# Cross attention of both layers: the last two query units and the four output units as seven products, one quarter of the output per unit

## What is computed

```python
def memory_cross_attention(h, mem_k, mem_v, wq, wo):
    q = (h @ wq).reshape(B, S, XATTN_HEADS, XATTN_HEAD_DIM)      # 4 heads of 256
    s = jnp.einsum('bshd,bmhd->bhsm', q, mem_k) * (XATTN_HEAD_DIM ** -0.5)
    p = jax.nn.softmax(s, axis=-1)
    o = jnp.einsum('bhsm,bmhd->bshd', p, mem_v).reshape(B, S, C)
    return o @ wo

for i in range(2):
    x = x + 0.5 * swiglu_ffn(rms_norm(x, ffn1_norm[i]), ...)
    h = rms_norm(x, mix_norm[i])
    x = x + (rwkv7_time_mix(h, ...) if i == 0 else gmlp_chunk_mix(h, ...))
    x = x + memory_cross_attention(rms_norm(x, xattn_norm[i]), mem_k, mem_v, wq[i], wo[i])
    x = x + 0.5 * swiglu_ffn(rms_norm(x, ffn2_norm[i]), ...)
```

## Time and profile before

| | us |
|---|---|
| median of 3 runs | 2095.15 |
| lowest and highest | 2095.09 and 2101.4 |
| the profiled execution, its own time | 2102.88 |
| its span in the trace | 2101.1 |
| TensorE busy | 2035.8 (97%) |
| VectorE busy | 1080.4 (51%) |
| ScalarE busy | 374.5 (18%) |
| GpSimd busy | 947.2 (45%) |

### The profile page before, as it was taken

How to read it: one execution, slowest core, us unless ns; L and a number is a source line. 1 busy time by engine, 2 the same in 40 slices (tenths; PEclk the granted TensorE clock), 3 DMA queues, 4 the chain that set the end, 5 groups by cost and what they waited for, 6 DMA issues and landing times.

```text
span 2101.1 us, 38775 instructions
## 1 busy us (share of the span) xinstructions
PE 2035.8 (97%) x16734; PEld 1900.8 (90%) x16734; DVE 1080.4 (51%) x1882; ACT 374.5 (18%) x769; POOL 947.2 (45%) x725
## 2 busy tenths in 40 slices
...
DMA packets 43588, 307.61 MB, mean 146 GB/s; under 512 B 5128, under 2 KB 5384, under 8 KB 7328
## 3 DMA queue, kind: packets, MB, share of 16 engines
...
## 4 chain that ended last, share of the span: by engine, by line
PE 92%; DVE 6%; issue 1%; ACT 1%; DMA 0%; SPq 0%; DVEq 0%; ACTq 0%
PE ps L541 53%; PE ps L252 16%; PE ps L304 8%; PE ps L249 3%; PE ps L266 3%; PE ps L281 1%; PE ps L1586 1%; DVE sb_xn L2406 1%; PE ps L360 1%; PE ps L1565 0%; DVE sb_xn L407 0%; PE ps L2135 0%; DMA sb_ring<-stream 0%; PE ps L2120 0%; PE ps L1991 0%
## 5 line engine op out<-in xcount | busy, mean ns | idle before, releaser
L541 PE MATMUL ps<-sb_work,sb_ring 128*128 128x128 f32 x3648 | 438.6, 275 | 2.0 <-DVE sb_work L1842 2.0
L541 PEld LDWEIGHTS ps<-sb_work,sb_ring 128*128 128x128 f32 x3648 | 423.1, 192 | 2.2 <-POOL sb_table L512 2.2
L512 POOL TENSOR_TENSOR sb_pad<-sb_ring 128x512 f32<-128x512 f32 x59 | 75.5, 1279 | 485.7 <-issue 318.9
L512 POOL TENSOR_TENSOR sb_table<-sb_ring 128x512 f32<-128x512 f32 x118 | 151.0, 1280 | 261.4 <-PE ps L541 152.6
L541 PE MATMUL ps<-sb_work,sb_table 128*128 128x128 f32 x2096 | 266.7, 275 | 0.0
L541 PEld LDWEIGHTS ps<-sb_work,sb_table 128*128 128x128 f32 x2096 | 250.6, 193 | 0.0
L515 POOL TENSOR_TENSOR sb_ring<-sb_ring 128x512 f32<-128x512 f32 x177 | 244.3, 1380 | 0.0
L541 PE MATMUL ps<-sb_xn,sb_ring 128*128 128x128 f32 x1376 | 167.7, 275 | 0.0
L514 POOL TENSOR_TENSOR sb_table<-sb_table,sb_ring 128x512 f32<-128x512 f32 x118 | 161.4, 1368 | 9.3
L304 PE MATMUL ps<-sb_work,sb_ring 128*128 128x256 f32 x736 | 160.1, 380 | 5.4 <-issue 1.9
L304 PEld LDWEIGHTS ps<-sb_work,sb_ring 128*128 128x128 f32 x736 | 139.4, 190 | 26.5 <-issue 4.4
...
## 6 DMA issues: line engine op xcount, KB each, us to landing
...
```

Source lines behind the costliest of these rows:

```text
L512: v.tensor_tensor(s[:, 0], a[1][0], a[1][1], ALU.add).then_inc(S["fw_ready"], 1)
L541: ins = mm(fast_bank(c, g, b)[:, i * P:i * P + P], *(sides[::-1] if token_major else sides), start=first and i == 0 and j == 0, stop=last ...
```

## The change

In each of the two layers, query units 2 and 3 and all four output units become fast units. The plan counts two banks instead of four for the queries. The list of stages that GpSimd prepares gets `l0_x` between `l0_ffn1` and `l0_ffn2`, and `l1_x` between `gm` and `l1_ffn2`; six units each. On VectorE, `spread_input` on `xn` now stands ahead of `rescaled`, and two `fast_sum` ahead of the first maximum; ScalarE makes two `copy_first` in place of two copies of a bank. Behind the last head VectorE makes for each head three differences of its output (`spread`, L1695, L1697 and L1699 of the changed kernel), written to `work[5]`. The output weights are cut the other way: each unit holds all 1024 inputs for 256 of the outputs, so a quarter of the result is complete with each unit, and `fast_residual` (L718) takes the place of `add_residual`: its sum in SBUF is added to `c.h` in SBUF.

```diff
@@ FAST_ORDER, fast_counts
-FAST_ORDER = ["b2_ffn", "l0_ffn1", "l0_ffn2", "l1_ffn1", "gm", "l1_ffn2"]
+FAST_ORDER = ["b2_ffn", "l0_ffn1", "l0_x", "l0_ffn2", "l1_ffn1", "gm", "l1_x", "l1_ffn2"]
...
+        elif name in ("l0_x", "l1_x"):
+            start, units, outs = PLAN[name + "q"][0] + 2, 6, 6
@@ fast_residual
+        if f is None and name != "gm_out":
+            c.wait_done(dve, PLAN[name][0] + b)
@@ xattn_tensor
     for u in range(2, 4):
-        p_unit(c, pe, n0 + u, q0 + u, c.xn)
+        pe.wait_ge(S["fw_ready"], 4 * (z0 + u - 2) + 4)
+        pe.wait_ge(S["fast_read"], g0 + u - 3)
+        fast_products(c, pe, n0 + u, z0 + u - 2, range(4),
+                      lambda k, j, t: c.xn[:, 2 * k + j, t * P:t * P + P], lambda k, m: xt[:, m, k, :],
+                      g0 + u - 2, True, True,
+                      (lambda: pe.wait_ge(S["spread"], x_count(i) + 4)) if u == 2 else None)\
+            .then_inc(S[f"unit_done{(n0 + u) % UNITS}"], 1)
...
                 pe.wait_ge(S["x_o_read"], 4 * i + hd - 1)
+                pe.wait_ge(S["spread"], x_count(i) + 4 + 3 * (hd - 2) + 3)
...
     pe.wait_ge(S["x_o_read"], 4 * i + 4)
+    pe.wait_ge(S["spread"], x_count(i) + 13)
     for u in range(4):
-        d_unit(c, pe, n0 + u, lambda k: W[1][:, 2 * u + k, :], u == 0, u == 3)
+        z, g = z0 + 2 + u, g0 + 2 + u
+        pe.wait_ge(S["fw_ready"], 4 * z + 4)
+        pe.wait_ge(S["fast_read"], g - 1)
+        fast_products(c, pe, n0 + u, z, range(4),
+                      lambda k, j, t: W[1][:, 2 * k + j, t * P:t * P + P],
+                      lambda k, m: x_spread(c, k)[:, m * P:m * P + P], g, True, True,
+                      (lambda: pe.wait_ge(S["spread"], x_count(i) + 16)) if u == 0 else None)\
+            .then_inc(S[f"unit_done{(n0 + u) % UNITS}"], 1)
@@ xattn_vector
+    dve.wait_ge(S["xn_ready"], 8 * NK[f"l{i}_x"] + 8)
+    spread_input(c, dve, c.xn, W[7], S["spread"], x_count(i))
     for u in range(2):
         rescaled(c, dve, f"l{i}_xq", u, W[0][:, 2 * u:2 * u + 2, :])
-    _, q0 = PLAN[f"l{i}_xq"]
+    for u in range(2, 4):
+        fast_sum(c, dve, g0 + u - 2, W[0][:, 2 * u:2 * u + 2, :].rearrange("p j t -> p (j t)"),
+                 lambda: c.wait_done(dve, n0 + u), ch)
...
-    add_residual(c, dve, f"l{i}_xo", PLAN[f"l{i}_xo"][0] + 3, 1.0, gain)
+    for hd in range(4):
+        spread(hd)
+    fast_residual(c, dve, f"l{i}_xo", None, 1.0, gain, ch)
@@ build, GpSimd
             pool.wait_ge(S["h_ready"], HR["rw_out"])
+            prepare_weights(c, pool, "l0_x")
             prepare_weights(c, pool, "l0_ffn2")
...
             prepare_weights(c, pool, "gm")
+            prepare_weights(c, pool, "l1_x")
             prepare_weights(c, pool, "l1_ffn2")
@@ kernel
-        units += p_units(a["xattn_wq_3"][i]) + d_units(a["xattn_wo_3"][i])
+        units += p_units(a["xattn_wq_3"][i]) + fast_d_units(a["xattn_wo_3"][i])
```

More of the change, by code:

```diff
@@ L469, in fast_counts @@
     for name in FAST_ORDER:
-        start, units, outs = (PLAN["gm_v"][0], 22, 18) if name == "gm" else \
-            (PLAN[name][0] + 2, 3 * FFI - 2, 2 * (FFI - 1) + 4)
+        if name == "gm":
+            start, units, outs = PLAN["gm_v"][0], 22, 18
+        elif name in ("l0_x", "l1_x"):
+            start, units, outs = PLAN[name + "q"][0] + 2, 6, 6
+        else:
+            start, units, outs = PLAN[name][0] + 2, 3 * FFI - 2, 2 * (FFI - 1) + 4
         first_unit_of[name], first_out[name] = len(unit_of), out
@@ L720, in fast_residual @@
     S, r = c.S, RESID.index(name)
-    g = FAST_G[name] + 2 * (FFI - 1) if f is not None else FAST_G["gm"] + 14
+    if name == "gm_out":
+        g = FAST_G["gm"] + 14
+    elif f is None:
+        g = FAST_G[name[:-1]] + 2
+    else:
+        g = FAST_G[name] + 2 * (FFI - 1)
     def complete(b):
-        if f is None:
+        if f is None and name != "gm_out":
+            c.wait_done(dve, PLAN[name][0] + b)
+        elif f is None:
             c.wait_done(dve, PLAN[name][0] + 2 * b + 1)
@@ L756 @@
 HR = {name: 4 * i + 4 for i, name in enumerate(RESID)}
-DPROJ = ["b1_out", "b2_out", "b2_ffn"] + [n for n in RESID[1:] if n != "gm_out"]
+DPROJ = ["b1_out", "b2_out", "b2_ffn"] + [n for n in RESID[1:] if n not in ("gm_out", "l0_xo", "l1_xo")]
 def b1_scalar(c, act):
@@ L1544, in ffn3, with x_spread @@
     return scalar, tensor, vector
+def x_spread(c, hd):
+    return c.work[5][:, 2 * hd:2 * hd + 2, :].rearrange("p j t -> p (j t)")
 def xattn_tensor(c, pe, i):
@@ L1561, in xattn_tensor @@
         if s < 4:
-            c.wait_read(pe, q0 + s)
+            if s < 2:
+                c.wait_read(pe, q0 + s)
+            else:
+                c.wait_read(pe, q0 + s - 4)
+                pe.wait_ge(S["fast_read"], g0 + s - 1)
             for n in range(2):
@@ L1601, in xattn_scalar @@
         rms_scalar(c, act, NK[f"l{i}_x"], r)
-    n0, q0 = PLAN[f"l{i}_xq"]
-    for u in range(2, 4):
-        c.wait_done(act, n0 + u)
-        c.read(nc.scalar.activation(W[0][:, 2 * u:2 * u + 2, :],
-                                    c.bank(q0 + u).rearrange("p (m t) -> p m t", m=2), ACT.Copy), q0 + u)
+    _, q0 = PLAN[f"l{i}_xq"]
+    g0 = FAST_G[f"l{i}_x"]
+    for u in range(2):
+        copy_first(c, act, g0 + u)
     for s in range(7):
@@ L1626, in xattn_scalar @@
             nc.scalar.activation(W[1][:, 2 * hd:2 * hd + 2, :],
-                                 c.ps[:, 7 - 3 * (hd % 2), :].rearrange("p (d q) -> p d q", d=2), ACT.Copy)\
+                                 c.ps[:, 4 + 3 * (hd % 2), :].rearrange("p (d q) -> p d q", d=2), ACT.Copy)\
                 .then_inc(S["x_o_read"], 1)
+    name = f"l{i}_xo"
+    for b in range(4):
+        copy_first(c, act, g0 + 2 + b)
+        act.wait_ge(S["h_ready"], 4 * RESID.index(name) + b + 1)
+        squares(c, NK[AFTER[name]], b, c.h)
 def xattn_vector(c, dve, i, ch, gain):
```

27 lines of the change are left out of this document (21 added, 6 removed).

## The result

The changed kernel took a median of 2101.14 us (20 runs, 2097.88 to 2105.31), the kernel before, run beside it, 2097.54 us (20 runs, 2094.65 to 2101.4). The ratio is **1.0015, 95% interval 1.0009 to 1.0021**, or 3.1 us more (1.9 to 4.4); the two medians stand 3.6 apart. That is a loss, but within the 0.3% that the prediction counts as no change. Forecast were +1.8 us, a median of 2097.0 and a range of 2091 to 2103.

A forecast was written before the change was run, and what follows sets the result against it. TensorE, busy 97% of the span, was taken as the bound. The terms -7.9 + 6.3 + 0.2 + 2.0 + 0 + 1.2 gave +1.8 us, a median of 2097.0 us, with a range of 2091 to 2103.

The forecast's parts named there:

- The saving: Both cross attentions: 12 ordinary units become fast ones, each 6.25 us instead of 6.905, 0.655 less; -7.9 us on TensorE.
- The start of layer 0: Layer 0's cross attention: early GpSimd preparations delay VectorE's L407, TensorE idles 4.1 us and its clock falls; +6.3 us.
- Layer 1's start: Layer 1's cross attention: GpSimd is through before L407, but late folds of squares make TensorE wait 0.21; +0.2 us.
- The attention: Behind the first score, two small VectorE scalings wait 0.3 and 1.0 for GpSimd; +1.0 us a layer, +2.0 together.
- The new waits: Ahead of the output units: three differences a head are ready in time or covered; 0, or 0.4 a layer if cover fails.
- The seams: From each cross attention to the next feed forward: the residual's SBUF operations meet GpSimd; +0.6 us a layer, +1.2 together.
- The sum: Whole kernel: all terms together give +1.8 us, a median of 2097.0 us.
- The collision stays small: Rival at layer 0's start: that term falls to about 0, giving 2090.7 us, or 2087.3 with others hidden; chance 0.15.
- The clock falls in the attention: Rival: the longer stop at the first transposes lowers the clock, costing 1.8 to 3.6 us a layer; chance 0.13.
- GpSimd becomes the bound of the output units: Rival: preparations take over 6.25 us, costing 0.5 a unit on eight units, +4 us, 2101; chance 0.07.

The follow-up runs named there:

- the run with all holds: Changed kernel with GpSimd preparations held by waits in both cross attentions, gm and three feed forwards, against the kernel before: ratio 0.994, 2086.19 us; repeated, 0.9931, 2085.18 us.
- the two half changes: Kernel before with only query units 2 and 3 fast: ratio 1.0001; with only the four output units fast: 1.0014; both layers each time.
- the outputs alone: Only the four output units of both layers fast, all query units ordinary, against the kernel before: ratio 1.0014 (1.0003 to 1.0025).
- the additions alone: Kernel before plus 12 unused GpSimd additions at layer 0's cross attention: 1.0034 when started at the finished `c.h`, 0.9997 when started behind the norm.

## Why the prediction was right

**The saving, -7.9.** Right. Query units 2 and 3 start 6.25 apart in layer 1, and with the collisions held off both layers are within 0.1 us of six times 0.655.

**The start of layer 0, +6.3.** The mechanism right, the size within 0.3. Measured +6.0, from the timelines of before and after. From the first unit to L252 it is 8.30 us instead of 7.77 (+0.5). From there to the first fast record 10.72 instead of 6.91 (+3.8, of it 3.65 idle). From there to the records behind the differences 3.49 instead of 1.79 (+1.7). Forecast were 4.1 idle, 0 ahead of it, and a low clock that hides the wait for the differences. The half microsecond ahead was missed: the squares and sums of the norm meet GpSimd too, not only L407, and TensorE waits 0.27 at L360. It doesn't always: of nine traces in which GpSimd starts at this place, four have this wait, and five have none. The two small errors, less idle time than forecast and half a microsecond ahead of it, cancel, and that is luck. L407 at 8.17 is near the forecast of 8.5.

**Layer 1's start, +0.2.** The wait right, its price wrong. TensorE waits 0.21 at L360, as in the earlier trace rows, but the next unit starts 8.25 us behind the first instead of 7.77: +0.5. The prediction took the 0.21 in brackets for the whole cost. The brackets count only from the modelled end of the last record, and matmuls are pipelined: without a stop the next record starts 0.16 before that end (7.07 long, 6.91 apart). From L360 to the next unit it is then 0.97 instead of 0.86. So a wait of 0.21 or 0.27 here costs about 0.5. The seam of the earlier trace rows shows the same price: 209.01 us with the wait, 208.53 in the run with all holds, without it.

**The attention, +1.0 a layer.** From the first score to output unit 0 it is 17.98 and 18.01 us instead of 17.21: +0.8. Forecast were waits of 0.3 and 1.0 at the two scalings; measured are 0.1 and 0.8 (0.29 and 0.94 long instead of 0.17).

**The new waits, 0.** Right: 0.69 ahead of the first output unit, as before, and no stop between the products.

**The seams, +0.6 a layer.** Measured +0.7: 0.5 by the wait of 0.27 at L360, and 0.16 within the first unit (7.23 instead of 7.07). What the prediction did not have is the seam of the two feed forwards behind: there the norm came 0.35 later than before although no line of it was changed. Timeline of the changed kernel, as in the earlier trace rows:

```profile
1437.33 0.69 DVE L385 TENSOR_TENSOR sb_work<-sb_work 128x512 f32<-128x512 f32 x1 [0.46 <-DVE sb_work L385]
1438.08 1.13 PE L360 MATMUL ps<-sb_work,sb_con 128*128 128x256 f32 x4 [0.56 <-DVE sb_work L385]
```

A gap of 0.46 stands between two folds on VectorE, and TensorE waits 0.56 instead of 0.21. The loss needs GpSimd's work at this place: with the third preparation of that stage held, the stretch is 208.53 instead of 209.36. But why it is 0.35 more than before is open: the two half changes have 209.00 there, the kernel before 209.01, and no run was made for the difference.

**The sum.** By the traces the stretches that begin at a changed place give +1.65, the open seam 0.35 more: +2.0 against +1.8 forecast. The times say +3.1, with an interval that begins at 1.9. The forecast median was also 2.4 low for another reason: it started from the three runs shown, whose median was 2095.15, and 20 runs of the same kernel give 2097.54. The mechanism and the large terms were right, but that the sum comes within 0.2 of the traces is partly luck: layer 1's start, the seams and the open seam were 0.8 too low together, the start of layer 0 and the attention 0.7 too high.

**The rivals.** *The collision stays small* is out: the changed kernel, the outputs alone and the additions alone show it in full. *The clock falls in the attention* did not occur; the two runs that hold only layer 0's second preparation there show that the mechanism exists, at a stop of 2.35. At 1.08 it did not come in this trace. *GpSimd becomes the bound of the output units* did not occur either: in layer 0 the four output units go from 1196.11 to 1221.22, 6.28 each, without a wait for prepared weights.

## What to carry over

When work is moved to an engine that shares SBUF with VectorE, don't ask only whether it has time. List what VectorE does at the moment when that work *becomes possible*: a preparation whose inputs are there early runs early, and 12 harmless additions beside the last step of a norm cost 6.5 us, a few microseconds later nothing. A wait placed in front of such work cost little here (0.41 in gm, where TensorE then waits for the second unit's weights), but look at where the held work lands, and hold what follows it too. A change that gives almost nothing may hide a gain of 8 and a loss of 10, and only the balance by stretches shows that. And read the price of a short wait from the distance between units, not from the idle time in brackets.

## What the runs showed of the chip beyond that

- A very small operation can wait for the end of a much larger one on the other engine: a scaling of 128x2 elements took 0.94 and 0.97 us beside GpSimd, 0.17 alone.
- A stop of TensorE of 3.65 to 4.55 us cost another 1.7 to 1.8 us behind it, at a granted clock of 0.52 in the changed kernel, whether fast or ordinary units followed.
- The same stop does not always bring the same clock. TensorE stops for 2.03 to 2.04 us at one place of gm in all twelve traces. The 16 records behind it take 2.02 us in seven of them, and 2.45 to 3.63 in the other five, at a low granted clock.
- Some of the noise of this kernel is the clock. In the windows below, the mixer of layer 0, with the same instructions in both kernels, took 478.5 us at a granted clock of 0.98 after the change, and 475.6 at 0.99 before it. In the other kernels' traces it took 472 to 479. A difference of 3 us can't be read from single runs.

Window of the changed kernel:

```profile
666.40:1144.90 478.50, 456.67 (x5454) 415.76 (x5454) 285.48 (x455) 95.78 (x186) 156.97 (x119) 0.98 0.32 114
```

and of the kernel before:

```profile
669.30:1144.90 475.60, 450.81 (x5453) 409.34 (x5453) 285.19 (x455) 95.84 (x186) 156.93 (x119) 0.99 0.32 115
```
